# Rotary embedding in a two-layer decoder step: the half swap on VectorE instead of a TensorE product

## The chip, the cores and the metric

One Trainium2 chip, one of its cores. The metric is the device time of one launch in microseconds (us); lower is better. All tensors are float32.

## What is computed

One step of a hybrid decoder trunk with two layers, for 1024 prompt tokens and 8 sample tokens (T = 1032 together), model width 1024. Each layer is an input projection, rotary embedding on queries and keys, sliding-window attention in blocks of 128 queries, a gated short convolution, an output projection with LayerNorm, a router and 32 experts with top-2 choice, and a second LayerNorm. The change lies in the rotary part of the projection:

```python
def rope(x, pos):
    half = HEAD_DIM // 2                       # HEAD_DIM = 64
    inv = ROPE_THETA ** (-jnp.arange(half) / half)
    ang = pos[:, None] * inv[None, :]
    cos, sin = jnp.cos(ang)[:, None, :], jnp.sin(ang)[:, None, :]
    x1, x2 = x[..., :half], x[..., half:]
    return jnp.concatenate([x1 * cos - x2 * sin, x2 * cos + x1 * sin], -1)

z = x @ w_in                                   # 2304 columns: q | k | v | B | C | h
q, k, v, gate_b, gate_c, h = jnp.split(z, cuts, axis=-1)
q = rope(q.reshape(bsz, n, 8, 64), pos)        # 8 query heads
k = rope(k.reshape(bsz, n, 2, 64), pos)        # 2 key heads
```

## The kernel before

The projection is made transposed: the 2304 columns are 18 tiles of 128 (`NTILE`), each computed as 128 partitions by 1032 tokens, and the tokens are cut into three chunks of 344 (`CH`, `NCH`). Tile 0 is the keys (two heads of 64 dimensions on 128 partitions), tiles 1 to 4 are the queries (two heads each), tile 5 the values, tiles 6 to 17 the inputs of the convolution in groups of three. So tiles 0 to 4 are rotated: five tiles, 15 chunks a layer, 30 chunks in all.

**TensorE.** `project(c, ...)` (L535 to L543) waits for the weights of tile c in one of three ring slots (`w_in0` to `w_in2`), then does for each chunk eight matmuls of 128x344 into one PSUM bank. Before each chunk it waits until ScalarE has emptied that bank two tiles ago (`act_ev`). `rotate(r)` (L545 to L552) multiplies the three chunks of tile r, as evicted to SBUF in `ztmp`, by the 128x128 matrix `rotm` (plus and minus ones that swap the two halves of 32 partitions in each head) into PSUM banks 6 and 7. It waits for `act_ev` of that chunk and, because there are two banks, for VectorE to have used the product two chunks ago (`rot_used`). The order is written out by hand: tile 0, tile 1, rotate 0, tile 2, rotate 1, ... tile 5, rotate 4, tile 6, tile 7, then the small matmuls of the sample attention after tiles 7, 8, 9 and 10, among the rest of the tiles. `sample_scores` after tile 7 waits for `smp_q` from GpSimd.

**ScalarE** copies each chunk from PSUM to SBUF (L918): tiles 0 to 4 into `ztmp`, which has two slots of a tile each. Before it overwrites a slot it waits until the rotation products and the cosine products of the tile two back are done (L923, L924).

**GpSimd** computes `zT = ztmp * cosT` for each chunk as it is evicted (L1581). When all 15 chunks are rotated (`rope_done`) and tile 5 is evicted, it prepares the sample queries and raises `smp_q`.

**VectorE** takes each product from PSUM, multiplies it by `sinT` into `rot` (L1120), waits for its own result and for `cos_done`, and adds `rot` to `zT` (L1124). After the 15 chunks it does sample steps and the convolution groups in a fixed order. `cosT` and `sinT` hold the angle of dimension d mod 32 on each partition, so all four groups of 32 partitions hold the same values.

**SyncE** issues the loads. Before the layers: x, the first three weight tiles, then 18 constants (`N_CONST`; `rotm` is the first, 64 KB) and a copy of x within HBM (4128 KB). In each layer: the convolution state, the LayerNorm rows `lnp` (2048 KB), the two caches (512 KB each), `wo` (4096 KB), and only behind those the weight tiles from tile 3 on (`w_tile`, L334 to L337, 512 KB each, issued when the tile three back is done).

After projection come attention and output projection block by block, then the experts in pairs, then the second LayerNorm; each stage hangs on semaphores of the one before.

Of the kernel before, what the change touches and what calls it, by code (L numbers as in the profile page):

```python
# [11 lines left out]
ALU = mybir.AluOpType  # L12
# [3 lines left out]
P = 128  # L16
# [7 lines left out]
NT = NB + 1  # L24
# [8 lines left out]
NTILE = 6 + 3 * CG  # L33
CH = T // 3
NCH = 3
# [13 lines left out]
BASE = 2  # L49
# [6 lines left out]
def settle(eng, passed):  # L56


    eng.sem_inc(passed, 1)
# [35 lines left out]
def build(nc, a):  # L95

    ctx = ExitStack()
    with ctx:
        def sb(name, shape, dt=F32):
            return ctx.enter_context(nc.sbuf_tensor(name, shape, dt))  # L100

        def sem(name):
            return ctx.enter_context(nc.semaphore(name))
# [3 lines left out]


        ident = sb("ident", [P, P])
        rotm = sb("rotm", [P, P])  # L110
        ones = sb("ones", [P, P])
        upper = sb("upper", [P, P])
        iota = sb("iota", [P, P])
        masks = sb("masks", [P, 3, 2 * P])
        cosT = sb("cosT", [P, T])
        sinT = sb("sinT", [P, T])
# [44 lines left out]
        def at(off, *shape, parts=P):  # L161
            n = int(np.prod(shape))
            v = arena[0:parts, off:off + n]
            if len(shape) == 2:
                return v.rearrange("p (a b) -> p a b", a=shape[0])
            if len(shape) == 4:
                return v.rearrange("p (a b c d) -> p a b c d", a=shape[0], b=shape[1], c=shape[2])
            if len(shape) == 3:
                return v.rearrange("p (a b c) -> p a b c", a=shape[0], b=shape[1])
            return v  # L170
# [6 lines left out]
        ztmp = at(21648, 2, T)  # L177
        rot = at(23712, 2, CH)
# [15 lines left out]
        def ws(off, *shape, parts=P):  # L194
# [57 lines left out]
        ps = ctx.enter_context(nc.psum_tensor("ps", [P, 8, 512], F32))  # L252

        s = {n: sem(n) for n in (
            "const_in", "init", "copied", "ident_in", "xin0", "xin1", "xt_mm", "xt_a", "xt_d", "x2_ready", "x2_out", "l2_stat", "l2_rstd",
            *(f"l2_in{t}" for t in range(NT)), "w_in0", "w_in1", "w_in2", "proj_mm", "act_ev", "rot_mm", "rot_used",
            "cos_done", "rope_done", "conv_done", "state_in", "state_set", "stage_done", "gate_staged", "v_t", "v_ev",
            "s_mm", "sm_ready", "p_ready", "pt_mm", "pt_ev", "pv_mm", "o_norm", "ot_mm", "ot_ev", "wo_in",
            "wo_mm", "xr_in0", "xr_in1", "ln_stat", "ln_rstd", "ln_add", "x1_ready",
            "x1_out0", "x1_out1", "x1t_mm", "x1t_a", "x1t_d", "rt_mm", "lg_ev", "lnp_in", "smp_in",  # L260
            "smp_q", "smp_s", "smp_max", "smp_p", "smp_n", "smp_t", "smp_pt", "smp_o", "smp_sel", "smp_ot", "smp_mix",
            "small_out", "rk_m", "rk_c", "rk_r", "rk_inv", "idx_ready", "rk_total", "rk_count", "rk_perm", "rk_order",
# [5 lines left out]
            "pe_passed", "dve_passed", "pool_passed", "sp_passed", "rk_exp", "rk_soft",  # L268
            "ys_free", "ov_xin", "ov_out", "ov_w", "ov_x", "ov_col", "ov_xt", "ov_xa", "ov_gu", "ov_silu", "ov_h", "ov_dn", "ov_y", "ov_sc")}

        N_CONST = 18
        block = ctx.enter_context(nc.Block())


# [4 lines left out]
                "x1_out1", "x2_out", "xin0", "xin1", "xr_in0", "xr_in1"),  # L279
            "tensor": (  # L280
                "dn_mm", "gu_mm", "ht_mm", "ot_mm", "ov_dn", "ov_gu", "ov_xt", "ov_inv", "proj_mm", "rk_count", "rk_order", "rk_turned", "rk_ranked", "pt_mm", "pv_mm", "rk_c", "rk_inv",
                "rot_mm", "rt_mm", "s_mm", "smp_o", "smp_ot", "smp_s", "smp_t", "v_t", "wo_mm", "x1t_mm", "xg_mm",
                "xt_mm"),
            "scalar": (
                "act_ev", "ht_a", "ot_ev", "ov_silu", "ov_xa", "p_ready", "pt_ev", "rk_exp", "silu",
# [18 lines left out]
        def _(sp):  # L304
            raise_to_base(sp, "sync")
            consts = [
                (rotm, a["c_rot"]), (upper, a["c_upper"]), (iota, a["c_iota"]),
                (masks, a["c_masks"]), (cosT, a["c_cos"]), (sinT, a["c_sin"]), (rank_desc, a["c_desc"]),
                (tokens1, a["c_tok1"]), (valid, a["c_valid"]), (sel8, a["c_sel8"]),
                (half_mask, a["c_half"]),  # L310
# [2 lines left out]
            for l in range(DEPTH):  # L313
                consts.append((wr[:, l], a["w_r"][l].rearrange("(k p) n -> p k n", p=P)))
                consts.append((br[:, l], a["b_r"][l].partition_broadcast(P)))
            assert len(consts) == N_CONST, len(consts)

# [28 lines left out]
            with sp.Fori(0, DEPTH) as l:  # L346
# [129 lines left out]
                for t in LN2_ORDER:  # L476
                    rows = P if t < NB else NS
                    r = slice(t * P, t * P + rows)
# [17 lines left out]
        def _(pe):  # L496
            raise_to_base(pe, "tensor")
            mm = nc.tensor.matmul
# [32 lines left out]
            with pe.Fori(0, DEPTH) as l:  # L531
# [3 lines left out]
                def project(c, slot, half, turn):  # L535

                    pe.wait_ge(s[f"w_in{slot}"], BASE + 16 * (6 * l + turn + 1))
                    for ch in range(NCH):
                        pe.wait_ge(s["act_ev"], BASE + (l * NTILE + c) * NCH + ch + 1)
                        for k in range(KD):  # L540
                            last = mm(ps[:, 3 * half + ch, 0:CH], wring[:, slot, k * P:(k + 1) * P],  # L541
                                      xT[:, k, ch * CH:(ch + 1) * CH], start=(k == 0), stop=(k == KD - 1))
                        last.then_inc(s["proj_mm"], 1)  # L543

                def rotate(r):  # L545

                    for ch in range(NCH):
                        i = NCH * r + ch
                        pe.wait_ge(s["act_ev"], BASE + (l * NTILE + r) * NCH + ch + 1 + 6)
                        pe.wait_ge(s["rot_used"], BASE + 15 * l + max(i - 1, 0))  # L550
                        mm(ps[:, 6 + i % 2, 0:CH], rotm[:], ztmp[:, r % 2, ch * CH:(ch + 1) * CH],  # L551
                           start=True, stop=True).then_inc(s["rot_mm"], 1)  # L552

                for c in range(6):
                    project(c, c % 3, c % 2, c // 3)
                    if c == 0:
                        pe.wait_ge(s["const_in"], BASE + 16 * N_CONST)
                        pe.wait_ge(s["init"], BASE + 6)
                    if c:
                        rotate(c - 1)  # L560

                def sample_scores():
                    pe.wait_ge(s["smp_q"], BASE + l + 1)
# [282 lines left out]
                with pe.If(pe.value_load(over[0:1, OVER:OVER + 1], min_val=0, max_val=OVER) > 0):  # L846
                    pe.wait_ge(s["ov_m"], BASE + l + 1)
                    settle(pe, s["pe_passed"])
                    for i in range(2 * NT):
                        last = mm(ps[:, 0, 0:2 * OVER], over_slot[:, i], over_block[:, i].rearrange("p q n -> p (q n)"),  # L850
                                  start=(i == 0), stop=(i == 2 * NT - 1))
# [6 lines left out]
                    with pe.Fori(0, OVER) as o:  # L858
                        n = OVER * l + o
                        pe.wait_ge(s["ov_xin"], BASE + n + 1)  # L860
                        for k in range(KD):
                            last = tr(ps[:, k // 4, (k % 4) * P:(k % 4 + 1) * P], xg_by_row[0][:, k], ident[:])
# [3 lines left out]
                        for f in range(FD):  # L866
                            for w, bank in ((wg, 2), (wu, 4)):
                                for k in range(KD):
                                    last = mm(ps[:, bank, f * P:(f + 1) * P], w[0][:, k, f * P:(f + 1) * P],
                                              xgT[:, 0, k], start=(k == 0), stop=(k == KD - 1))  # L870
                        last.then_inc(s["ov_gu"], 1)
                        pe.wait_ge(s["ov_h"], BASE + n + 1)
                        for h in range(2):
                            for f in range(FD):
                                last = mm(ps[:, 6 + h, :], hT[:, f], wd[0][:, f, h * 512:(h + 1) * 512],
                                          start=(f == 0), stop=(f == FD - 1))
# [16 lines left out]
        def _(act):  # L893
# [18 lines left out]
            with act.Fori(0, DEPTH) as l:  # L912

                def evict(c, half, dst):
                    for ch in range(NCH):
                        n = (l * NTILE + c) * NCH + ch
                        act.wait_ge(s["proj_mm"], BASE + n + 1 + 6)
                        nc.scalar.copy(dst[:, ch * CH:(ch + 1) * CH], ps[:, 3 * half + ch, 0:CH]  # L918
                                       ).then_inc(s["act_ev"], 1)

                for c in range(5):

                    act.wait_ge(s["rot_mm"], BASE + 15 * l + max(c - 1, 0) * NCH)  # L923
                    act.wait_ge(s["cos_done"], BASE + 15 * l + max(c - 1, 0) * NCH)  # L924
                    evict(c, c % 2, ztmp[:, c % 2])
                evict(5, 1, zT[:, 5])
# [134 lines left out]
        def _(dve):  # L1061
            raise_to_base(dve, "vector")
            v = nc.vector
# [20 lines left out]
            dve.wait_ge(s["init"], BASE + 6)  # L1084
            dve.wait_ge(s["const_in"], BASE + 16 * N_CONST)
            settle(dve, s["dve_passed"])
# [26 lines left out]
            with step.loop(DEPTH, STEPS_LAYER) as l:  # L1113

                for r in range(5):
                    for ch in range(NCH):
                        i = NCH * r + ch
                        cols = slice(ch * CH, (ch + 1) * CH)
                        dve.wait_ge(s["rot_mm"], BASE + 15 * l + i + 1)
                        v.tensor_tensor(rot[:, i % 2], ps[:, 6 + i % 2, 0:CH], sinT[:, cols], ALU.mult  # L1120
                                        ).then_inc(s["rot_used"], 1)
                        dve.wait_ge(s["rot_used"], BASE + 15 * l + i + 1)
                        dve.wait_ge(s["cos_done"], BASE + 15 * l + i + 1)
                        v.tensor_tensor(zT[:, r, cols], zT[:, r, cols], rot[:, i % 2], ALU.add  # L1124
                                        ).then_inc(s["rope_done"], 1)
# [442 lines left out]
        def _(pool):  # L1568
            raise_to_base(pool, "gpsimd")
            g = nc.gpsimd  # L1570
            step = Steps(pool, s["pool_step"], s["pool_passed"])
            pool.wait_ge(s["const_in"], BASE + 16 * N_CONST)
            pool.wait_ge(s["init"], BASE + 6)
# [263 lines left out]
```

## Time and profile before

| | |
|---|---|
| median of 3 runs | 2474.08 us (2473.35, 2474.08, 2480.47) |
| the profiled execution, device time | 2476.03 us |
| its span in the trace | 2474.2 us |
| mean granted TensorE clock | 0.941 |
| busy: TensorE, VectorE, ScalarE, GpSimd | 92%, 24%, 14%, 13% |
| projections (L541) in the chain that ended last | 20% |

Durations in the trace are from one execution. A float32 matmul shows as two records: the 864 projection matmuls stand as 1728, the 30 rotation products as 60. The ends of matmuls are modelled, so the distance from one start to the next tells more than the duration of one record. Rows of a timeline or of the chain are merged: a row gives the start, the time to the end of the last, and the count.

### The profile page before, as it was taken

How to read it: one execution, taken by the hardware profiler on the slowest of the kernel's cores; microseconds unless marked ns; L12 is line 12 of the kernel's file. 1: busy time of each engine (PE TensorE's matmuls, PEld its weight loads, DVE VectorE, ACT ScalarE, POOL GpSimd, SP SyncE). 2: the span in 40 equal slices, each digit the busy share in tenths (PEclk: the TensorE clock that was granted, in tenths of full speed). 3: DMA queues.
4: the chain of work that ended last, by engine and by line, in shares of the span. 5: the costliest groups of instructions: out<-in, count | busy, mean ns of one | idle time of the engine just before them, and what ended most of it. 6: DMA issues, size and time to landing. Idle time of an engine off the chain costs nothing.

```text
span 2474.2 us, 30238 instructions
## 1 busy us (share of the span) xinstructions
PE 2266.5 (92%) x10256; PEld 1518.3 (61%) x10256; DVE 602.2 (24%) x1207; ACT 334.1 (14%) x827; POOL 324.4 (13%) x440
## 2 busy tenths in 40 slices
PE   7999899996999999999589998999879999999994
PEld 5666556655666666666356665665556666666662
DVE  1111254444111111111421112443521111111115
ACT  2000032220101111111110001222101111111111
POOL 0100011100111111111311000110111111111113
PEclk9999997897999999999789998987979999999996
DMA  7311011124899999999341110211358999999973
GB/s 245 114 37 40 14 60 51 51 110 179 311 387 374 374 379 368 376 374 350 137 172 35 34 43 10 73 43 44 149 231 314 375 384 368 379 374 373 371 265 142
DMA packets 101742, 526.40 MB, mean 213 GB/s; under 512 B 16298, under 2 KB 25514, under 8 KB 84930
## 3 DMA queue, kind: packets, MB, share of 16 engines
q1 hardware_dynamic: 86818, 491.58, 51.2%
q0 software_dynamic: 14848, 33.85, 5.5%
q8 instruction: 42, 0.69, 0.1%
q14 instruction: 34, 0.28, 0.0%
HBM read 489.95 MB, written 58.27 MB: 222 GB/s over the span
## 4 chain that ended last, share of the span: by engine, by line
PE 87%; DVE 5%; issue 4%; DMA 2%; ACT 1%; DVEq 0%; POOL 0%; SPq 0%; POOLq 0%; ACTq 0%
PE ps L783 21%; PE ps L541 20%; PE ps L816 10%; PE ps L663 9%; PE ps L787 8%; PE ps L820 4%; PE ps L607 3%; PE ps L766 3%; PE ps L627 2%; PE ps L683 1%; PE ps L673 1%; DVE arena L1553 1%; DVE arena L1443 1%; PE ps L551 1%; DVE stat L1546 1%
## 5 line engine op out<-in xcount | busy, mean ns | idle before, releaser
L783 PE MATMUL ps<-arena 128*128 128x256 f32 x2304 | 511.3, 383 | 2.5 <-DVE arena L1443 2.5
L541 PE MATMUL ps<-arena 128*128 128x344 f32 x1728 | 507.7, 455 | 4.9 <-issue 4.1
L783 PEld LDWEIGHTS ps<-arena 128*128 128x128 f32 x2304 | 438.8, 192 | 88.0 <-issue 28.9
L541 PEld LDWEIGHTS ps<-arena 128*128 128x128 f32 x1728 | 329.6, 191 | 177.4 <-issue 9.2
L816 PE MATMUL ps<-arena 128*128 128x512 f32 x576 | 255.8, 597 | 21.0 <-ACT arena L1011 19.9
L663 PE MATMUL ps<-arena 128*128 128x512 f32 x512 | 237.8, 624 | 2.9 <-DVE arena L1258 2.9
L1669 POOL DMA_INDIRECT ytok<-arena,scol x64 | 98.7, 1542 | 974.5 <-DVE arena L1467 618.7
L1454 DVE SCALAR_TENSOR_TENSOR arena<-ps,gates,arena 128x256 f32<-128x256 f32 (+1 forms) x128 | 61.5, 481 | 665.5 <-ACT arena L1006 665.5
L787 PE MATMUL ps<-arena 128*64 128x256 f32 x896 | 199.4, 381 | 0.0
L789 PE MATMUL ps<-arena 128*64 128x256 f32 x896 | 199.4, 381 | 0.0
L816 PEld LDWEIGHTS ps<-arena 128*128 128x128 f32 x576 | 106.5, 190 | 149.0 <-issue 122.1
L663 PEld LDWEIGHTS ps<-arena 128*128 128x128 f32 x512 | 101.4, 201 | 132.0 <-issue 132.0
L787 PEld LDWEIGHTS ps<-arena 128*64 128x64 f32 x896 | 120.4, 137 | 81.9 <-issue 21.2
L1467 DVE COPY arena<-ps 128x512 f32<-128x512 f32 x64 | 44.3, 692 | 372.6 <-PE ps L816 263.9
L1006 ACT ACTIVATE arena<-ps 128x256 f32<-128x256 f32 (+1 forms) x128 | 49.0, 383 | 624.0 <-PE ps L783 453.1
L789 PEld LDWEIGHTS ps<-arena 128*64 128x64 f32 x896 | 120.4, 137 | 0.0
L512 PE MATMUL ps<-ident,arena 128*128 128x128 f32 (+1 forms) x216 | 49.6, 406 | 77.1 <-DVE arena L1556 63.9
L820 PE MATMUL ps<-arena 128*64 128x512 f32 x224 | 101.3, 595 | 18.5 <-DVE arena L1460 18.5
L918 ACT COPY arena<-ps 128x344 f32<-128x344 f32 x108 | 48.2, 446 | 480.4 <-PE ps L541 437.4
L822 PE MATMUL ps<-arena 128*64 128x512 f32 x224 | 102.1, 599 | 0.0
L512 PEld LDWEIGHTS ps<-ident,arena 128*128 128x128 f32 (+1 forms) x216 | 40.5, 223 | 86.9 <-issue 78.6
L1018 ACT COPY arena<-ps 128x512 f32<-128x512 f32 x64 | 37.3, 583 | 388.1 <-PE ps L816 275.5
(220 smaller groups left out, 1845.8 us busy)
## 6 DMA issues: line engine op xcount, KB each, us to landing
arena<-in_w_gate SPq DMA_DIRECT2D x64, 2048.0 KB
arena<-in_w_up SPq DMA_DIRECT2D x64, 2048.0 KB
arena<-in_w_down SPq DMA_DIRECT2D x64, 2048.0 KB, 17.7
arena<-in_w_in SPq DMA_DIRECT2D x36, 512.0 KB, 3.3
arena<-in_w_o SPq DMA_DIRECT2D x2, 4096.0 KB, 19.4
arena<-out_y_all SPq DMA_DIRECT2D x16, 512.0 KB, 3.2
xs<-arena SPq DMA_DIRECT2D x16, 512.0 KB, 2.6
ytok<-arena SPq DMA_DIRECT2D x16, 512.0 KB, 3.8
```

Of the source, the lines that this page charges most:

```text
L512: last = tr(ps[:, 2 * slot + k // 4, (k % 4) * P:(k % 4) * P + rows], src[0:rows, k * P:(k + 1) * P], ident[0:rows, 0:rows])
L541: last = mm(ps[:, 3 * half + ch, 0:CH], wring[:, slot, k * P:(k + 1) * P], xT[:, k, ch * CH:(ch + 1) * CH], start=(k == 0), stop=(k == KD ...
L607: last = mm(ps[:, 2 * h + j // 2, (j % 2) * 256:(j % 2) * 256 + 256], qs[h * HD:(h + 1) * HD, slot, j], kwin[h * HD:(h + 1) * HD, :], star ...
L663: last = mm(ps[0:rows, 6 + n, :], mix[:, k, 0:rows], wo[:, k, n * 512:(n + 1) * 512], start=(k == 0), stop=(k == KD - 1))
L766: last = tr(ps[:, k // 4, (k % 4) * P:(k % 4) * P + rows], xg_by_row[slot][0:rows, k], ident[0:rows, 0:rows])
L783: last = mm(ps[:, 2 + q, at_c:at_c + 256], xgT[:, slot, k], w[slot][:, k, cols], start=(k == 0), stop=(k == KD - 1))
L787: mm(ps[HALF:P, 2 + q, 0:256], xgT[:, slot, k, 0:HALF], wg[slot][:, k, cols], start=(k == 0), stop=(k == KD - 1))
L789: last = mm(ps[0:HALF, 2 + q, 0:256], xgT[:, slot, k, 0:HALF], wu[slot][:, k, cols], start=(k == 0), stop=(k == KD - 1))
L816: last = mm(ps[:, 6 + h, :], hT[:, f], wd[slot][:, f, h * 512:(h + 1) * 512], start=(f == 0), stop=(f == FD - 1))
L820: mm(ps[0:HALF, 6, :], hT[:, f, 0:HALF], wd[slot][:, f, 0:512], start=(f == 0), stop=(f == FD - 1))
L822: last = mm(ps[HALF:P, 7, :], hT[:, f, 0:HALF], wd[slot][:, f, 512:DM], start=(f == 0), stop=(f == FD - 1))
L1669: g.indirect_dma_start(out=a["ytok"][0], out_offset=bass.IndirectOffsetOnAxis(ap=scol[0:rows, slot:slot + 1], axis=0), in_=ys[0:rows, slot ...
```

## The change

The rotation matrix, its load, its semaphore and its products go. VectorE waits for ScalarE's eviction of the chunk itself and builds `rot` in four passes of 32 partitions: pass q reads `ztmp` and `sinT` on the neighbouring 32 partitions (q ^ 1), multiplies them with each other and with the constant minus one or plus one, and writes to partitions 32q to 32q + 31 of `rot`. The addition that follows is unchanged. ScalarE waits for `rot_used` (VectorE's passes done) where it waited for `rot_mm` (the products done) before it reuses a slot of `ztmp`.

```diff
-        rotm = sb("rotm", [P, P])
...
-        N_CONST = 18
+        N_CONST = 17
...
             consts = [
-                (rotm, a["c_rot"]), (upper, a["c_upper"]), (iota, a["c_iota"]),
+                (upper, a["c_upper"]), (iota, a["c_iota"]),
...
-                def rotate(r):
-
-                    for ch in range(NCH):
-                        i = NCH * r + ch
-                        pe.wait_ge(s["act_ev"], BASE + (l * NTILE + r) * NCH + ch + 1 + 6)
-                        pe.wait_ge(s["rot_used"], BASE + 15 * l + max(i - 1, 0))
-                        mm(ps[:, 6 + i % 2, 0:CH], rotm[:], ztmp[:, r % 2, ch * CH:(ch + 1) * CH],
-                           start=True, stop=True).then_inc(s["rot_mm"], 1)
-
                 for c in range(6):
                     project(c, c % 3, c % 2, c // 3)
                     if c == 0:
                         pe.wait_ge(s["const_in"], BASE + 16 * N_CONST)
                         pe.wait_ge(s["init"], BASE + 6)
-                    if c:
-                        rotate(c - 1)
...
-                    act.wait_ge(s["rot_mm"], BASE + 15 * l + max(c - 1, 0) * NCH)
+                    act.wait_ge(s["rot_used"], BASE + 15 * l + max(c - 1, 0) * NCH)
                     act.wait_ge(s["cos_done"], BASE + 15 * l + max(c - 1, 0) * NCH)
...
-                        dve.wait_ge(s["rot_mm"], BASE + 15 * l + i + 1)
-                        v.tensor_tensor(rot[:, i % 2], ps[:, 6 + i % 2, 0:CH], sinT[:, cols], ALU.mult
-                                        ).then_inc(s["rot_used"], 1)
+                        dve.wait_ge(s["act_ev"], BASE + (l * NTILE + r) * NCH + ch + 1 + 6)
+                        for q in range(4):
+                            to, of = slice(32 * q, 32 * q + 32), slice(32 * (q ^ 1), 32 * (q ^ 1) + 32)
+                            last = v.scalar_tensor_tensor(rot[to, i % 2], ztmp[of, r % 2, cols], 2.0 * (q % 2) - 1,
+                                                          sinT[of, cols], ALU.mult, ALU.mult)
+                        last.then_inc(s["rot_used"], 1)
                         dve.wait_ge(s["rot_used"], BASE + 15 * l + i + 1)
                         dve.wait_ge(s["cos_done"], BASE + 15 * l + i + 1)
                         v.tensor_tensor(zT[:, r, cols], zT[:, r, cols], rot[:, i % 2], ALU.add
```

## Rows read from the trace of the kernel before

**Rows 1.** The page, part 1: busy us (share of span), instructions.
```profile
PE 2266.5 (92%) x10256; PEld 1518.3 (61%) x10256; DVE 602.2 (24%) x1207; ACT 334.1 (14%) x827; POOL 324.4 (13%) x440
```

**Rows 2.** Chain that ended last: start us, us, engine, line; both projections.
```profile
30.25 29.41 PE ps L541 x96
61.69 13.88 PE ps L541 x48
77.61 13.88 PE ps L541 x48
...
125.35 27.76 PE ps L541 x96
...
1253.30 30.57 PE ps L541 x96
1285.90 13.88 PE ps L541 x48
```

**Rows 3.** Groups by line and shape: busy us, mean ns, idle before and releaser.
```profile
L541 PE MATMUL ps<-arena 128*128 128x344 f32 x1728 | 507.7, 455 | 4.9 <-issue 4.1 <-DVE arena L1075 0.9
...
L551 PE MATMUL ps<-arena,rotm 128*128 128x344 f32 x60 | 21.7, 470 | 0.3
...
L1120 DVE TENSOR_TENSOR arena<-ps,sinT 128x344 f32<-128x344 f32 x30 | 15.3, 510 | 154.3 <-PE ps L551 154.3
```

**Rows 4.** Timeline, first rotated tile: start us, us, engine, line, [idle before, releaser].
```profile
59.50 2.20 PE L551 MATMUL ps<-arena,rotm 128*128 128x344 f32 x6
59.70 0.45 ACT L918 COPY arena<-ps 128x344 f32<-128x344 f32 x1 [4.18 <-PE ps L541]
60.22 0.92 POOL L1581 TENSOR_TENSOR arena<-arena,cosT 128x344 f32<-128x344 f32 x1 [3.71 <-ACT arena L918]
60.28 0.52 DVE L1120 TENSOR_TENSOR arena<-ps,sinT 128x344 f32<-128x344 f32 x1 [15.12 <-PE ps L551]
60.83 0.68 DVE L1124 TENSOR_TENSOR arena<-arena 128x344 f32<-128x344 f32 x1
...
61.97 0.52 DVE L1124 TENSOR_TENSOR arena<-arena 128x344 f32<-128x344 f32 x1
```

**Rows 5.** Groups by line and shape, VectorE: one operation on 128 and 8 partitions.
```profile
L1231 DVE SCALAR_TENSOR_TENSOR arena<-arena,mv,lnp 128x1024 f32<-128x1024 f32 x16 | 20.6, 1285 | 0.6
...
L1231 DVE SCALAR_TENSOR_TENSOR arena<-arena,mv,lnp 8x1024 f32<-8x1024 f32 x2 | 2.5, 1273 | 0.1
```

**Rows 6.** Timeline, SyncE's DMA issues in layer 0: start us, us, line, tensors.
```profile
55.55 5.64 SPq L359 DMA_DIRECT2D arena<-in_w_o  x1
61.80 78.00 SPq L337 DMA_DIRECT2D arena<-in_w_in  x7
```

**Rows 7.** L337, landing: issues of 61.8; of 75.8 to 107.6; of 1270.2 and 1284.1.
```profile
DMA to landing us min/median/max: 14.1/14.1/14.1
...
DMA to landing us min/median/max: 3.3/3.3/3.6
...
DMA to landing us min/median/max: 4.0/5.8/7.5
```

**Rows 8.** Stretches: us; busy of PE, PEld, DVE, ACT, POOL; clock, DMA share, GB/s.
```profile
70.00:75.00 5.00, 5.00 (x19) 3.31 (x18) 0.00 (x0) 0.45 (x1) 0.91 (x1) 1.00 1.04 415
75.00:80.00 5.00, 4.97 (x17) 2.98 (x17) 3.08 (x6) 0.45 (x1) 0.91 (x1) 1.00 0.42 142
```

**Rows 9.** Timeline, layer 0: the sample queries on GpSimd, their first use on TensorE.
```profile
127.30 0.58 POOL L1591 MEMSET sample_ws<- 128x576 f32 x1 [17.94 <-DVE arena L1124]
...
153.04 1.99 PE L566 MATMUL ps<-arena,sample_ws 128*64 128x129 f32 x16
```

**Rows 10.** Timeline of TensorE: first work of attention and of the experts, by layer.
```profile
306.55 0.47 PE L601 MATMUL ps<-ident,arena 128*128 128x128 f32 x1 [9.10 <-POOLq L1614]
...
597.85 2.50 PE L783 MATMUL ps<-arena 128*128 128x256 f32 x5 [1.27 <-DVE arena L1443]
...
1530.76 0.47 PE L601 MATMUL ps<-ident,arena 128*128 128x128 f32 x1 [9.10 <-POOLq L1614]
...
1820.16 15.20 PE L783 MATMUL ps<-arena 128*128 128x256 f32 x58 [1.27 <-DVE arena L1443]
```

More of the change, by code:

```diff
@@ L255, in build @@
             "const_in", "init", "copied", "ident_in", "xin0", "xin1", "xt_mm", "xt_a", "xt_d", "x2_ready", "x2_out", "l2_stat", "l2_rstd",
-            *(f"l2_in{t}" for t in range(NT)), "w_in0", "w_in1", "w_in2", "proj_mm", "act_ev", "rot_mm", "rot_used",
+            *(f"l2_in{t}" for t in range(NT)), "w_in0", "w_in1", "w_in2", "proj_mm", "act_ev", "rot_used",
             "cos_done", "rope_done", "conv_done", "state_in", "state_set", "stage_done", "gate_staged", "v_t", "v_ev",
@@ L281, in build @@
                 "dn_mm", "gu_mm", "ht_mm", "ot_mm", "ov_dn", "ov_gu", "ov_xt", "ov_inv", "proj_mm", "rk_count", "rk_order", "rk_turned", "rk_ranked", "pt_mm", "pv_mm", "rk_c", "rk_inv",
-                "rot_mm", "rt_mm", "s_mm", "smp_o", "smp_ot", "smp_s", "smp_t", "v_t", "wo_mm", "x1t_mm", "xg_mm",
+                "rt_mm", "s_mm", "smp_o", "smp_ot", "smp_s", "smp_t", "v_t", "wo_mm", "x1t_mm", "xg_mm",
                 "xt_mm"),
```

## The prediction, made before the changed kernel was run

> **What bounds the kernel now.** I read four views, in this order. First the busy shares: TensorE is busy for 92% of the span, VectorE for 24% [rows 1]. That says where to look and nothing yet about this stage. Second, the chain of work that ended last, at both projections. There every step is a projection matmul, from 30.25 us in layer 0 and from 1253.30 us in layer 1 [rows 2]. The reader is to see the rhythm: a tile whose neighbour needs no rotation takes 13.88 us (27.76 for 96 records is 13.88 for 48), while the tiles between which a rotation stands start 15.92 us apart (61.69 to 77.61). Third, the groups by line: the projection matmuls waited for something for only 4.9 us in 1728 records, and VectorE's sine product sat idle for 154.3 us until a rotation product came [rows 3]. So TensorE sets the pace, and the engine that is to take the work over waits for TensorE nearly all the time. Fourth, SyncE's issues and their landing times, because a stage that gets faster asks for its weights sooner [rows 6 to 8].
>
> **What the change removes on TensorE.** One rotation block is three products, six records. From the start of the block at 59.50 [rows 4] the next projection matmul in the chain stands at 61.69, which also holds the end of the last matmul of tile 1; its net cost is better read from two starts: 77.61 - 61.69 - 13.88 = 2.04 us. Another reading: tiles 0 and 1 end at 30.25 + 29.41 = 59.66 and tile 2 begins at 61.69, 2.03 us; in layer 1, 1253.30 + 30.57 = 1283.87 and 1285.90, 2.03 us [rows 2]. There are five blocks a layer and two layers: 10 x 2.03 = 20.3 us. This includes the wait for VectorE to free a bank. Nothing lies beside it, since TensorE runs one stream. If no other wait takes its place the span falls by 20.3 us.
>
> **What it adds on VectorE.** A chunk costs now one product (0.51 us, [rows 3]) and one addition (0.52, or 0.68 when GpSimd's cosine product runs at the same time, [rows 4]). Afterwards it costs four passes and the addition. No row has a pass of 344 columns on 32 partitions that writes to other partitions. From below: the two-input operations of 344 columns take 0.51 to 0.52 us, and fewer partitions don't make an operation shorter: 1024 columns took 1285 ns on 128 partitions and 1273 ns on 8 [rows 5]. From above: that same operation at 1024 columns, with a pointer scalar, took 1.29 us; a pass of a third of the columns shouldn't cost more than that unless crossing partitions has a price of its own. I take 0.52 us, because the row of the same width is the nearest. A chunk is then 4 x 0.52 + 0.56 + about 0.1 for the wait on its own result = 2.7 us, and 30 chunks add 30 x 3 x 0.52 = 47 us to VectorE's busy time. It all lies beside TensorE: a chunk comes every 4.63 us (13.88 / 3), so VectorE ends each chunk before the next one is evicted. The end of the range, 4 x 1.29 + 0.56 + 0.1 = 5.8 us, is over 4.63 but hidden too, as the rival below works out.
>
> GpSimd's cosine product (0.92 us) starts 0.52 us after ScalarE's copy starts [rows 4], and so will VectorE's first pass. Today only one addition in three meets it and takes 0.68 instead of 0.52 us, so 0.16 us more for 0.31 us of overlap (60.83 to 61.14); at that rate 0.92 us of overlap costs a chunk about 0.5 us, and it becomes 3.2. Both products read two SBUF inputs. The Trainium skill (SBUF — State Buffer, section "SBUF: two separate sides") says that such a VectorE operation and a GpSimd operation that reads SBUF share a port pair as an exclusive lock: one waits until the other is through. By that rule a chunk would be 2.7 + 0.9 = 3.6 us. The row speaks of a smaller price than a full wait; by either the chunk stays below 4.63 us, and only the distance to the slower rival shrinks. The Trainium skill (VectorE: DVE Perf Modes, section "Two Vector instructions with no wait between them") also says that an operation starting on other partitions than the last one is held until that one is finished; each of the four passes is such a one. No pair of this trace does that, so I count full durations, with no overlap of neighbours.
>
> **Waits that change.** ScalarE now waits, before tile c goes to `ztmp`, for VectorE's passes of tile c - 2 instead of TensorE's products. Behind that wait stands the eviction, and behind it TensorE's tile c + 2. The passes of tile c - 2 end some 3 us after its last eviction, over ten us before tile c's first: cost zero, and that cover is a whole tile. VectorE's new wait on `act_ev` has nothing queued behind it but the rest of the rotation and the sample steps. The rotated tiles are complete sooner: GpSimd starts the sample queries now at 127.30, after waiting for the last addition, and TensorE wants them at 153.04 [rows 9], so it had 26 us to spare and will have more. The constant load of 64 KB goes: one issue less on SyncE, about 0.5 us, ahead of everything that follows there.
>
> **What is late next.** The weights of tile 3 in layer 0. They are queued behind the 4096 KB of `wo`, whose issue holds SyncE's queue from 55.55 to 61.2; tile 3 is issued at 61.80 [rows 6] and lands 14.1 us later, at 75.9, where an undisturbed tile takes 3.3 [rows 7]. The DMA engines are at 415 GB/s until 75 us and then fall to 142 [rows 8]: this is a backlog of bytes that TensorE's pace doesn't move. Today tile 3 starts at 77.61, 1.7 us later than its weights. After the change tile 2 starts where the first rotation stands now, at 59.50, and ends at 59.50 + 13.88 = 73.4. The weights land at 75.9 less the 0.5 us of the missing issue = 75.4, so TensorE waits 2.0 us, once. Bounds: nothing, if the missing constant and issue bring the landing forward by 2 us; 2.5, if they bring nothing. I take 2.0, because SyncE's queue and the engines were full from one issue to the next. Tile 4 is issued next to it and is needed 14 us later. In layer 1 tile 3 lands at 1270.2 + 7.5 = 1277.7 at the latest [rows 7], and is wanted at 1283.87 + 13.88 = 1297.8: no wait.
>
> **The sum.** 20.3 - 2.0 = 18.3 us off. The profiled span of 2474.2 us becomes 2455.9 and its device time of 2476.03, which lies 1.8 us above the span, becomes 2457.7. The median of the runs shown is 2474.08, 1.95 us below the profiled time, so I predict 2474.08 - 18.3 = 2455.8 us. Behind the projection everything is counted from its end: attention begins 9.10 us after it, in both layers, on the convolution and GpSimd's staging [rows 10], and these hang on the last tiles. I cost the move of the later stages at nothing, with one reserve. The stretches at the lower of the two clock levels in attention don't lie at the same place in both layers: from the first transpose of attention to the first expert matmul it is 291.3 us in layer 0 (597.85 - 306.55) and 289.4 in layer 1 (1820.16 - 1530.76) [rows 10]. A stage that starts elsewhere can so win or lose about 2 us, each layer.
>
> **Rivals.**
> (a) The weights come in time. For it: the queue gets shorter by one issue and 64 KB. Against it: 2.0 us are missing and 0.5 are given. Time 2474.08 - 20.3 = 2453.8. Chance 0.1.
> (b) More is given back in waits and clock than I count. The wait of 2 us for tile 3 could let the clock fall; at the start of layer 1, where TensorE comes out of idleness at half clock, the first two tiles take 30.57 instead of 27.76 us, 2.8 us more [rows 2]. With that, or with 2 us lost in the attention of each layer, it is 2455.8 + 2.8 to 2455.8 + 6.8, middle 2460. Against the clock: the stretch of 70 to 75 us is at 1.00 [rows 8] and full work lies on both sides of the wait. Chance 0.15.
> (c) VectorE becomes the bound, and the kernel slower. The place is `sample_scores` after tile 7, which waits for GpSimd, which waits for the last rotation. In layer 0 VectorE can begin near 45 us and TensorE ends tile 7 at 59.50 + 6 x 13.88 + 2.0 = 144.8. GpSimd needs about 3 us between. So 15 chunks have 97 us, 6.4 us each; with 0.66 for addition and wait that is a pass of 1.45 us. Above it each further microsecond of a chunk costs 15 us a layer. The gain of 18.3 us is used up at about 0.6 us more a chunk, a pass of 1.6 us, three times the row. At twice that excess, 1.75 us a pass, the time is 2474 + 18 = 2492. For it: no row shows a pass that crosses partitions. Against it: no duration in rows 3 to 5 comes near for this width. Chance 0.03.
> (d) The edit gives nothing: the stages behind don't move with the projection, say because a transfer sets the start of the experts. Time 2474. Against it: attention starts at the same 9.10 us behind both projections [rows 10], released by engines. Chance 0.04.
>
> **How the numbers follow.** The forecast (18.3 us off) has 0.68. What a measurement of this kernel can tell from no change is about 0.3%, 7.4 us. The forecast, (a) and (b) are all beyond it; only the bad end of (b) comes near. So faster 0.92, same 0.04, slower 0.04. The range takes in (a), two stages that win 2 us each, (b), and the spread of the runs shown, one of which lies 6.4 us above the median: 2450 to 2464.
>
> **What would show it.** No record of L551. Tiles 1 to 7 of a projection start 13.88 us apart, but for one gap of about 2 us ahead of tile 3 in layer 0, put down to the DMA of the weights, and the landing near 75.4. Four passes of about 0.52 us per chunk, VectorE's busy time up by some 47 us, the last addition of layer 0 ending near 106 us (59.50 + 3 x 13.88 + 2.0 + 0.5 + 2.7) instead of 127. ScalarE's evictions every 4.63 us without a wait for VectorE. Wrong would be: passes over 1.45 us; a TensorE wait ahead of tile 7's sample work; a longer gap at the head of attention; or several microseconds more at the lower clock behind the tile 3 wait.

## The result, and the profile after

The changed kernel has a median of 2459.18 us over 4 runs (2452.12 to 2461.83), beside 2474.7 (2473.35 to 2480.47) for the kernel before. The medians are 15.5 us apart. The ratio, which goes by all the runs and not by the two medians, is 0.9928, with a 95% interval of 0.9902 to 0.9955, so 17.8 us less (11 to 24). The forecast was 2455.8 us, a ratio of 0.9926, and the time lies in the stated range, on its slower side. The profiled execution took 2452.12 us with a span of 2450.3, which is 23.9 us under the span of before: more than was forecast, and more than the medians differ. Most of what follows is about that difference.

The busy line of the page, after (against [rows 1]):

```profile
PE 2243.5 (92%) x10196; PEld 1505.3 (61%) x10196; DVE 664.9 (27%) x1297; ACT 334.0 (14%) x827; POOL 333.3 (14%) x440
```

TensorE lost 60 records and 23 us, VectorE gained 90 instructions and 62.7 us. The chain that ended last, after (start us, us, line; against [rows 2]), shows the projections without their interruptions:

```profile
75.81 69.66 PE ps L540 x240
...
1237.62 112.93 PE ps L540 x384
```

Five tiles take 69.66 us, 13.93 each, and the first eight tiles of layer 1 go through in one piece of 112.93 us. Before, the same eight tiles with their five rotation blocks took from 1253.30 to 1377.31, 124.0 us.

The rotation in the changed kernel: groups by line and shape (busy us, mean ns, idle before; against [rows 3]), then its timeline (start us, us; against [rows 4]):

```profile
L1110 DVE SCALAR_TENSOR_TENSOR arena<-arena,sinT 32x344 f32<-32x344 f32 x120 | 78.5, 654 | 48.7 <-ACT arena L906 47.1 <-DVE cols L1091 0.2
L1572 POOL TENSOR_TENSOR arena<-arena,cosT 128x344 f32<-128x344 f32 x30 | 36.3, 1209 | 149.2 <-ACT arena L906 107.8 <-DMA br<-in_b_r 41.4
```

```profile
50.21 2.07 DVE L1110 SCALAR_TENSOR_TENSOR arena<-arena,sinT 32x344 f32<-32x344 f32 x4
...
61.09 0.45 ACT L906 COPY arena<-ps 128x344 f32<-128x344 f32 x1 [4.18 <-PE ps L540]
61.56 2.70 DVE L1110 SCALAR_TENSOR_TENSOR arena<-arena,sinT 32x344 f32<-32x344 f32 x4 [1.37 <-ACT arena L906]
61.61 1.24 POOL L1572 TENSOR_TENSOR arena<-arena,cosT 128x344 f32<-128x344 f32 x1 [3.39 <-ACT arena L906]
64.30 0.52 DVE L1115 TENSOR_TENSOR arena<-arena 128x344 f32<-128x344 f32 x1
...
107.07 0.52 DVE L1115 TENSOR_TENSOR arena<-arena 128x344 f32<-128x344 f32 x1
```

Four passes take 2.07 us where GpSimd is silent and 2.70 us where its cosine product runs beside them, and then VectorE waits 1.4 us for the next eviction. The last addition of layer 0 is at 107.07. The reader should compare the 4.18 us that ScalarE waits for TensorE before each eviction with the same number in [rows 4]: the eviction rhythm is TensorE's, not VectorE's.

The wait ahead of tile 3, in TensorE's timeline, and its weights' landing (the issue at 60.63; against [rows 7]):

```profile
30.11 44.82 PE L540 MATMUL ps<-arena 128*128 128x344 f32 x144 [0.85 <-DVE arena L1063]
75.81 4.60 PE L540 MATMUL ps<-arena 128*128 128x344 f32 x15 [0.88 <-DMA arena<-in_w_in]
```

```profile
DMA to landing us min/median/max: 15.0/15.0/15.0
```

The weights landed at 75.67 and tile 3 started at 75.81. The issue came 1.2 us earlier than in the kernel before (61.80), the landing only 0.2 us earlier (75.9): the landing doesn't follow the issue.

To see where the time went I cut every trace at four marks in each layer. The stages run from the first projection matmul to the first transpose of attention, from there to the first expert matmul, and from there to the second LayerNorm's first transpose. In us (before / after): projection 276.3 / 268.8 and 277.5 / 266.4; attention 291.3 / 284.5 and 289.4 / 293.3; experts 618.8 / 618.6 and 618.4 / 617.7; second LayerNorm of layer 0 to the next projection 36.7 / 35.6. The projections give 18.6 us. Attention, which the change doesn't touch, gives 6.8 and takes 3.9, so 2.9 in sum. The rest of the 23.9 us, some 2.4, lies in the experts, the second LayerNorm and the start, which the change doesn't touch either.

### The profile page after: what moved, and what is told of

Same layout as the page of the kernel before. It is cut to its first block, busy times and chain, and to the rows that moved or that the text cites. A ratio compares the mean times of both kernels' runs of the same rounds, so it can differ in the third digit from the quotient of the medians.

```text
span 2450.3 us, 30176 instructions
## 1 busy us (share of the span) xinstructions
PE 2243.5 (92%) x10196; PEld 1505.3 (61%) x10196; DVE 664.9 (27%) x1297; ACT 334.0 (14%) x827; POOL 333.3 (14%) x440
## 4 chain that ended last, share of the span: by engine, by line
PE 85%; DVE 6%; issue 4%; DMA 2%; SPq 1%; ACT 1%; DVEq 0%; POOL 0%; POOLq 0%; ACTq 0%
PE ps L771 21%; PE ps L540 19%; PE ps L804 10%; PE ps L651 9%; PE ps L775 8%; PE ps L808 4%; PE ps L595 3%; PE ps L754 3%; PE ps L615 2%; PE ps L671 1%; PE ps L661 1%; DVE arena L1544 1%; DVE arena L1434 1%; DVE stat L1537 1%; PE ps L606 1%
## 5 line engine op out<-in xcount | busy, mean ns | idle before, releaser
L804 PE MATMUL ps<-arena 128*128 128x512 f32 x576 | 255.8, 597 | 20.3 <-ACT arena L999 19.2
L1110 DVE SCALAR_TENSOR_TENSOR arena<-arena,sinT 32x344 f32<-32x344 f32 x120 | 78.5, 654 | 48.7 <-ACT arena L906 47.1
```

What stands on the lines that cost most here:

```text
L804: last = mm(ps[:, 6 + h, :], hT[:, f], wd[slot][:, f, h * 512:(h + 1) * 512], start=(f == 0), stop=(f == FD - 1))
L1110: last = v.scalar_tensor_tensor(rot[to, i % 2], ztmp[of, r % 2, cols], 2.0 * (q % 2) - 1, sinT[of, cols], ALU.mult, ALU.mult)
```

## The experiments

**Two traces more, with nothing changed: does attention belong to the kernel or to the execution?** The kernel before again:

> The kernel before, unchanged, for a second trace. Theory A (the clock in attention falls where it likes, from execution to execution): the two projections keep their lengths of 276.3 and 277.5 us (first projection matmul to first attention transpose) within 2 us, but the two attention stages (first attention transpose to first expert matmul), 291.3 and 289.4 us in the first trace, come out different by several us. Rival B (the lengths belong to the kernel and to where its stages start): both come out within 0.5 us of 291.3 and 289.4.

Projections 276.8 and 277.6 us; attention 295.0 and 285.8. The changed kernel again, in twelve runs:

> The changed kernel, unchanged, for a tighter ratio and a second trace. Its first trace had projections of 268.8 and 266.4 us and attention stages of 284.5 and 293.3 us. Theory A (execution to execution): projections again within 2 us of these, so 17 to 20 us less than before in sum, attention stages different by several us, and the median over many runs about 17 us below before, ratio 0.992 to 0.994. Rival B: attention again 284.5 and 293.3, and the median nearer to the 24 us that the first trace shows, ratio 0.990.

Median 2453.19 us (2443.76 to 2467.0) beside 2474.66 (2455.01 to 2483.36, 19 runs), ratio 0.9924 (0.9896 to 0.9951), which is 18.8 us less; the medians are 21.5 us apart. Projections 267.7 and 267.7, attention 289.5 and 289.8. A third time, as the base of the last four kernels:

> The changed kernel, unchanged, as the comparison for the other three on the same chip. Projections of 266 to 269 us each; the two attention stages anywhere from 284 to 295 us, longer the more of the stage is at the lower clock. Ratio to before 0.992 to 0.994.

Median 2451.78 us (2445.26 to 2471.1), beside 2474.24 (2457.18 to 2482.45, 23 runs), ratio 0.9937 (0.9911 to 0.9962), 15.6 us less, with medians 22.5 us apart; projections 268.5 and 266.4, attention 279.5 and 290.3. The 279.5 lies outside the 284 to 295 that were expected. So the projections keep their lengths within about 1.3 us and attention varies by 14 us in one and the same kernel. Theory A holds for the lengths of the stages. The size of the gain is less sharp: the ratios of the three series say 17.8, 18.8 and 15.6 us, their medians 15.5, 21.5 and 22.5. The stretches of attention show what goes with it (us, busy of PE, PEld, DVE, ACT, POOL, granted clock, DMA share, GB/s). Layer 0 of the kernel before in its second trace:

```profile
306.90:601.92 295.02, 264.31 (x1151) 171.09 (x1152) 136.66 (x294) 60.76 (x180) 31.46 (x54) 0.84 0.24 91
```

layers 0 and 1 of the changed kernel in its first trace:

```profile
298.91:583.38 284.47, 253.97 (x1152) 165.17 (x1152) 136.67 (x294) 60.71 (x180) 31.51 (x54) 0.87 0.25 95
1503.99:1797.27 293.28, 262.05 (x1151) 170.05 (x1152) 136.71 (x294) 60.71 (x180) 31.36 (x54) 0.85 0.25 92
```

and layer 0 of its third:

```profile
299.42:578.94 279.52, 248.49 (x1151) 162.64 (x1152) 136.59 (x294) 60.71 (x180) 31.41 (x54) 0.89 0.26 96
```

The busy time of VectorE, ScalarE and GpSimd is equal within 0.2 us; TensorE's time and its granted clock move, and they move together: 0.84 at 295 us, 0.89 at 279.5. Why the clock is lower in one execution than in another isn't shown.

**The wait for tile 3.** The edit lets `wo` go behind the weight tiles:

```diff
-                sp.dma_start(wo, a["w_o"][l].rearrange("(k p) n -> p k n", p=P)).then_inc(s["wo_in"], 16)
                 with sp.Fori(0, NTILE // 3 - 1) as i:
                     for slot in range(3):
                         w_tile(NTILE * l + 3 * i + slot + 3, slot)
+                sp.dma_start(wo, a["w_o"][l].rearrange("(k p) n -> p k n", p=P)).then_inc(s["wo_in"], 16)
```

> The changed kernel, with the 4096 KB load of wo issued behind all weight tiles of the layer. Theory (tile 3 of layer 0 waits for its bytes behind wo): tile 3's weights land before 66 us, TensorE has no wait for in_w_in, and the first projection is shorter by that wait, 0.9 to 2 us; the second projection is unchanged at 266.4. Time 1 to 2 us below the changed kernel, which is at the edge of what can be told. Rival (the gap ahead of tile 3 has another cause): the gap of 0.9 us or more stays. A second rival: wo is now late for the output projection, and attention begins later by up to 20 us.

The chain shows the first eight tiles of layer 0 in one piece:

```profile
28.91 114.23 PE ps L540 x384
```

Tile 3 was issued at 56.12 and landed 8.0 us later, at 64.1; there was no wait for `in_w_in` ahead of tile 3; attention still began 9.10 us after the projection. The projections took 267.7 and 267.3 us. Median 2449.31 us (2433.91 to 2453.7), ratio 0.9915 (0.9884 to 0.9946). The wait is gone, which shows its cause. The projection isn't shorter for it than the 267.7 us of the changed kernel's second trace, and layer 1 is 0.9 longer than the 266.4 expected: in both layers some ten matmuls at the start came at the low clock. A second series beside the third of the changed kernel, on the same chip:

> The load of wo behind the weight tiles, on the same chip as the changed kernel. Theory (it takes away the wait for tile 3, 0.4 to 0.9 us in the traces so far, and nothing else): no wait for in_w_in ahead of tile 3, medians within 2 us of the changed kernel. Rival (the 3.9 us between the medians of the first two series is real): 3 to 5 us below it.

Median 2449.46 us (2441.61 to 2458.44) against 2451.78, ratio to before 0.991 (0.9886 to 0.9934); projections 266.8 and 266.3, again without the wait. By medians the two series are 3.9 and 2.3 us better than the changed kernel beside them, by ratios 2 and 7 us. The 2.3 lies between what theory (within 2) and rival (3 to 5) had expected and decides for neither, and in both series the intervals overlap: this order is the best kernel of the study by its medians, but its lead isn't shown. In the kernel before, the same order:

> The kernel before with the same reordering of wo. Theory: there tile 3's weights land 1.7 us before they are wanted, so the first projection stays at 276.3 us within 0.5 (apart from how long the clock stays low at its start). Rival (the early weights help by something else, such as less DMA traffic): it shortens by 1 us or more, as in the changed kernel.

Projections 277.4 and 277.4 us, 1.1 longer in layer 0 and equal in layer 1. Its first two tiles took 30.51 us instead of 29.41 (low clock at the start), which is that 1.1. With the products in place there was no wait to remove. The kernel had one run, of 2475.31 us.

**How much VectorE work fits.** The four passes done twice or three times, the extra ones into a scratch buffer:

```diff
+                        for q4 in range(8):            # 4 for twice
+                            q = q4 % 4
+                            to, of = slice(32 * q, 32 * q + 32), slice(32 * (q ^ 1), 32 * (q ^ 1) + 32)
+                            v.scalar_tensor_tensor(acc[to, CH * (q4 // 4):CH * (q4 // 4) + CH], ztmp[of, r % 2, cols], 2.0 * (q % 2) - 1,
+                                                   sinT[of, cols], ALU.mult, ALU.mult)
```

> The changed kernel with the four passes done twice, the first time into a scratch buffer: eight passes and the addition a chunk, about 8 x 0.52 + 0.6 (with GpSimd at the same time) + 0.6 = 5.4 us, longer than the 4.63 us between two evictions. Theory (hidden until the sample step after tile 7 asks for the rotated tiles, which allows 6.4 us a chunk): time as the changed kernel within 3 us, both projections within 1 us of 268.8 and 266.4. Rival (VectorE must keep up with each eviction): 0.8 us x 15 chunks x 2 layers = 23 us longer.

Median 2456.18 us (2451.47 to 2462.02) beside 2472.8, ratio 0.9928 (0.9908 to 0.9948), the same as the changed kernel; projections 268.0 and 266.4. From its first pass (45.21) to its last addition VectorE needed 5.3 us a chunk. Additions of the last tile came 4.74 us apart, a little slower than evictions, the last at 124.27, and the sample scores started at 144.26 without a wait.

> The same with the passes done three times: about 12 x 0.52 + 0.6 + 0.6 = 7.5 us a chunk, over the bound of 6.4. Theory: TensorE waits ahead of the sample scores after tile 7, 44 + 15 x 7.5 + 3 - 145.5 = 14 us in layer 0 and 1245 + 112.5 + 3 - 1350.5 = 10 us in layer 1, so about 25 us more than the changed kernel, near 2483. ScalarE's evictions of tiles 3 and 4 come late, without a wait on TensorE. Rival (the cover is larger, the sample step isn't the place): as the changed kernel. Rival (keep up with each eviction): 2.9 x 30 = 86 us more.

Median 2478.62 us (2470.69 to 2493.11), ratio 1.0033 (0.9999 to 1.0067), with 7.4 us a chunk in the trace. All of the gain is gone. TensorE's waits name the place (total us, times, longest):

```profile
PE ps L554 <- POOLq L1595: 20.5, 2, 11.3
```

L554 is the sample scores after tile 7, which waited 11.3 us in layer 0 and 9.2 in layer 1; 14 and 10 had been expected. The first is short because tile 7 itself ended about 3 us later than reckoned, which is the next finding. ScalarE waited 70.6 us for VectorE in all, and no projection matmul waited for it. The two waits cost more than their own 20.5 us, which the expectation didn't count: behind them the granted clock was 0.50, the sample scores took 3.70 us instead of 1.99, and the next tile 15.21 us in layer 0 instead of 14.08.

**What the wait does to the clock.** In that trace TensorE waited 2.42 us for tile 3, up to 77.53. In the second trace of the kernel with the later cosine product (below) it waited 2.79, up to 77.73. The stretches around both, three passes first:

```profile
75.00:78.00 3.00, 0.58 (x2) 0.47 (x2) 2.92 (x5) 0.45 (x1) 1.08 (x1) 0.87 0.91 329
78.00:81.00 3.00, 3.00 (x7) 1.72 (x7) 2.90 (x7) 0.00 (x0) 0.00 (x0) 0.56 0.10 36
```

```profile
75.00:78.00 3.00, 0.27 (x1) 0.28 (x2) 2.45 (x5) 0.42 (x1) 0.37 (x1) 1.00 0.96 341
78.00:81.00 3.00, 3.00 (x11) 1.92 (x11) 0.61 (x2) 0.00 (x0) 0.91 (x1) 1.00 0.07 23
```

After the shorter wait the clock fell for a few microseconds from full to half (2.4 to 1.2 GHz), and only 7 matmul records stand in the next 3 us instead of 11; after the longer one it stayed up. The trace with three passes lost about 1.5 us so (tiles 3 to 7 took 148.72 - 77.53 = 71.2 us instead of 69.66). In the seven other traces with this wait, of 0.19 to 1.74 us, the matmuls behind it kept the spacing of the full clock, 0.29 us. The Trainium skill (TensorE: Matmul & The Clock Gate, section "HAM oscillation — how this bites in real kernels") describes such a fall around waits for DMA; the first of these traces agrees in kind, and the second shows that a wait of this size need not do it.

**Do passes across partitions cost more?** Each pass reads its own 32 partitions (`(q ^ 1)` becomes `q`), which leaves out the swap:

> The changed kernel with each of the four passes reading its own 32 partitions, so the halves are not swapped (this leaves out the swap). Theory (crossing partitions has no price of its own): four passes take 2.07 us without GpSimd beside them and 2.70 with it, as in the changed kernel. Rival (crossing costs): less than 2.0 us without GpSimd.

Its timeline at the start, where GpSimd is silent:

```profile
49.57 2.07 DVE L1110 SCALAR_TENSOR_TENSOR arena<-arena,sinT 32x344 f32<-32x344 f32 x4
```

The same 2.07 us, and about 2.70 beside GpSimd; 2455.14 us in one run. Crossing has no price of its own here.

**What makes 2.07 into 2.70?** GpSimd waits for VectorE's passes:

```diff
-                        pool.wait_ge(s["act_ev"], BASE + (l * NTILE + r) * NCH + ch + 1 + 6)
+                        pool.wait_ge(s["rot_used"], BASE + 15 * l + NCH * r + ch + 1)
                         g.tensor_tensor(zT[:, r, cols], ztmp[:, r % 2, cols], cosT[:, cols], ALU.mult
```

> The changed kernel with GpSimd's cosine product waiting for VectorE's passes of the chunk instead of for the eviction, so that the two don't run at the same time. Theory (the 0.63 us that four passes cost more in most chunks is GpSimd's product beside them): all groups of four passes take 2.07 us, the cosine product 0.91 instead of 1.24 us, the chunk is not shorter, since the addition now waits for the cosine product, and the time is that of the changed kernel. Rival (the long passes come from something else, such as TensorE's or ScalarE's reads of the same tiles): groups of 2.70 us stay.

```profile
60.23 2.07 DVE L1110 SCALAR_TENSOR_TENSOR arena<-arena,sinT 32x344 f32<-32x344 f32 x4
62.38 0.92 POOL L1572 TENSOR_TENSOR arena<-arena,cosT 128x344 f32<-128x344 f32 x1 [2.80 <-DVE arena L1110]
63.40 0.52 DVE L1115 TENSOR_TENSOR arena<-arena 128x344 f32<-128x344 f32 x1 [1.10 <-POOL arena L1572]
```

All 120 passes are short (mean 508 ns) and so is the product (mean 915 ns). The cause is the product beside the passes. Within a group of the changed kernel it is one pass that pays. The one that starts at 62.1, while GpSimd's product of 61.61 to 62.85 runs:

```profile
L1110 DVE SCALAR_TENSOR_TENSOR arena<-arena,sinT x1: 1130/1130/1130, 62.1 to 62.1; 32x344 f32<-32x344 f32 x1
```

1.13 us instead of 0.51, ending 0.4 us after the product; the other three are 0.50 to 0.51. The first of them began 0.05 us before the product and wasn't slowed: the product paid, with 1.24 us instead of 0.92. The kernel with the later product took 2470.25 us in its one run, 15 more than expected, with projections of 268.5 and 266.3 and attention stages of 299.2 and 294.2. So it got a series of runs:

> GpSimd's cosine product behind VectorE's passes, timed. In its one trace the projections were as short as those of the changed kernel (268.6 and 266.3), but the attention stages 299.2 and 294.2 us. Theory A (chance of one execution; the edit touches nothing in attention): the median is within 2 us of the changed kernel. Rival (the edit shifts the start of attention to a place where the clock is lower more often): the median is 10 us or more above it again, and attention again above 294.

Median 2459.15 us (2446.35 to 2467.64), ratio 0.995 (0.993 to 0.997), and attention 284.9 and 289.1 in its second trace. So the long attention doesn't belong to the kernel. The median is still 7.4 us above the changed kernel's, which neither theory (within 2) nor rival (10 or more) had expected; by the ratios, 0.995 against 0.9937, it is 3 us. The projections are 269.9 and 266.4, which explains 1.4. The intervals overlap, and whether the rest is real stays open.

**Would less VectorE work help?** One pass over 128 partitions instead of four, which leaves out swap and sign:

> The four passes replaced by a single pass over all 128 partitions, which reads its own partitions (this leaves out the swap and the sign). VectorE has 3 x 0.52 us less to do in each of 30 chunks. Theory (the passes are hidden beside TensorE): projections of 266 to 269 us, median within 2 us of the changed kernel. Rival (VectorE's extra work costs something, by its reads or by the clock): the median is 3 us or more below the changed kernel.

Median 2451.6 us (2441.37 to 2456.56), ratio 0.9925 (0.9898 to 0.9953); projections 268.3 and 267.6. The same as the changed kernel, as far as these series can tell (3 us apart by the ratios, 0.2 by the medians): no cost of the passes on the path is to be seen.

## Why the prediction was right, point by point

**The products' 20.3 us** stood. Layer 1 shows it clean: the first eight tiles need 11.1 us less, of which 0.9 is a shorter start at the low clock (112.93 - 111.04 = 1.9 us above eight times 13.88, before 2.8), and 10.2 the five blocks. In layer 0 of the changed kernel this low clock can be read: from 30 to 36 us the granted clock is 0.50, and the first matmul records start 0.57 us apart instead of 0.29. In sum the projections took 553.8 and 554.5 us in two traces of before and 535.2, 535.4 and 535.0 in three of after: 18.9 us less, where 18.3 was forecast. That the sum came out so near is in part luck. In the first trace the wait cost 1.1 us less than forecast, while the low clock at the start, put at no change, cost 1.5 us more in layer 0 and 0.9 less in layer 1; these nearly cancel.

**The wait for tile 3** is there, with the cause named and shown by removing it. The landing was forecast for 75.4 and measured at 75.7. The wait itself was mis-sized: 2.0 forecast, 0.88 in the first trace. The step behind it that failed is the start of tile 2 at 59.50, and with it its end at 73.4, which came at 74.9: in this execution the low clock at the start of the projection lasted longer and cost 3.2 us in the first three tiles (44.82 - 41.64), 1.5 more than in the trace of before (29.41 - 27.76 = 1.65), so TensorE came later to tile 3 and waited less. In nine traces of the changed kernel and its variants with `wo` ahead of the tiles the wait was between 0.19 and 2.79 us. It absorbs what is lost or won before it: the landing sets the start of tile 3. The landing moves too, from 74.5 to 77.6 us, which is more than the end of tile 2 moves (73.5 to 75.5).

**VectorE's cost.** 0.52 us a pass was right; the upper bound of 1.29 was far too wide. The price of GpSimd's product was put at 0.5 us a chunk from the row. It is 0.63: one pass pays, the others are untouched, and GpSimd pays 0.33 as well (1.24 against 0.91). The exclusive lock of the Trainium skill (SBUF — State Buffer, section "SBUF: two separate sides") had given 0.9 and has the form right, but it isn't exact: the product is 0.33 us longer where it overlaps the first pass by 0.46, and the second pass ends 0.37 us after the product where a whole pass takes 0.51. VectorE's busy time rose by 62.7 us rather than 47, the 0.63 us in most chunks being what was left out of that sum. The four passes take 2.07 us together, 0.52 from start to start and none overlapping. That is what the Trainium skill's rule on held instructions says (VectorE: DVE Perf Modes, section "Two Vector instructions with no wait between them"); passes on their own partitions also start elsewhere each time and were no quicker, so no run here shows the other side of that rule. The last addition was forecast to end near 106 and ended at 107.6.

**Rival (c)**, VectorE as the bound at the sample scores from 6.4 us a chunk on, is right in place, and the threshold fits: 5.3 us a chunk changed nothing, 7.4 us a chunk brought the wait there and took the whole gain. No run lies near 6.4, but both lead to it. At 5.3 us the last addition ended 19.5 us before the sample scores, of which GpSimd needs about 3, so some 16 us or 1.1 a chunk were left. At 7.4 us the wait of 11.3 us is 0.75 a chunk, which leaves 6.6, with a tile 7 that was itself 3 us late (0.2 a chunk). The prediction had it from the timeline alone.

**Rival (b), the clock**, was right as a mechanism and wrong in size for attention. Its first half, that the wait for tile 3 lets the clock fall, came in one of nine traces, although full work lay on both sides of the wait, which the prediction held against it. Two stages of one trace, 291.3 and 289.4 [rows 10], suggested 2 us either way. Traces of the changed kernel show 279.5 to 293.3, those of before 285.8 to 295.0. In the first pair attention gave 2.9 of the 5.3 us by which the spans differ more than the projections. The runs of before spread over 28 us in a longer series, the fastest at a mean granted clock of 0.951 and the slowest at 0.939; that this lies in attention is likely and not shown, as these runs have no trace. The prediction put what a measurement can tell at about 0.3%. For a series against a series that is about right (the intervals are some 0.25% to each side), for one run against another it is far too little.

## What to carry to other kernels

A product with a permutation matrix of 32-partition blocks takes TensorE's time like any other, here 2.03 us for three chunks; where TensorE is the bound and VectorE idle for most of each eviction period, as here, four shifted passes cost nothing that could be measured. Before moving work to an idle engine, find the first consumer that must have it and divide the time until then by the number of pieces: here 6.4 us a chunk, not the 4.6 between evictions. When a stage gets shorter, look at which load was just in time for it: the next wait is written in the landing times of before.

## What the runs showed of the hardware

- An operation on 32 partitions that reads one group of 32 and writes another takes what an operation of its width takes: 0.51 us for 344 columns, 0.52 from start to start, the same as without crossing.
- VectorE with two SBUF inputs and GpSimd's two-input product hold each other up one instruction at a time: 1.13 us for one pass, 0.51 for its neighbours. Who starts second pays: the product itself took 1.24 us instead of 0.92.
- The same code's attention stage lasts from 279.5 to 293.3 us, with a mean granted clock of 0.89 to 0.85. A comparison by one trace each is worth no more than that; stages that the change touches must be compared by themselves.
- Behind a wait of 2.42 us TensorE's granted clock fell once, and behind one of 2.79 us in another execution it didn't. Behind waits of 9.2 and 11.3 us it was 0.50, and 16 small matmuls took 3.7 us instead of 2.0.
